# A mixture-of-experts trunk: row gathers issued two double blocks ahead, light experts begun at the sixth double block, ranking split over three steps

## The reference, cut to what matters

```python
def swiglu(h, wg, wu, wd):
    return (jax.nn.silu(h @ wg) * (h @ wu)) @ wd

def moe_swiglu(h, router, eg, eu, ed):
    t = h.reshape(b * s, d)                       # 256 x 1024
    logits = (t @ router).astype(jnp.float32)
    top_v, top_i = lax.top_k(logits, TOP_K)       # 2 of 8
    top_w = jax.nn.softmax(top_v, axis=-1)
    combine = jnp.sum(jax.nn.one_hot(top_i, N_EXPERTS) * top_w[..., None], axis=1)
    for e in range(N_EXPERTS):
        out = out + combine[:, e:e + 1] * swiglu(t, eg[e], eu[e], ed[e])
    return out
```

## Time and profile before

| | |
|---|---|
| median of 3 runs | 1368.14 us (1366.64 to 1369.67) |
| the profiled execution | 1369.39 us, span of the profile 1367.6 us |
| TensorE (PE) busy | 1323.7 us, 97% (a matmul's row includes its drain) |
| VectorE (DVE) busy | 1121.4 us, 82% |
| ScalarE (ACT) busy | 942.1 us, 69% |
| mean granted TensorE clock | 0.991 |
| chain that ended last | PE 76%, DVE 14%, DMA 5%, ACT 3% |
| DMA | 438.27 MB, mean 320 GB/s over the span; 362 to 422 GB/s in the slices from 513 to 1333 us |

### The profile page before, as it was taken

The page is one execution under the profiler, slowest core; times in us unless marked ns, Lnnn a source line. Parts: engine busy times, 40 slices in busy tenths (PEclk is TensorE's granted clock), DMA queues, the critical chain, the costliest instruction groups (busy, mean ns, idle before and its releaser), DMA issues.

```text
span 1367.6 us, 17501 instructions
## 1 busy us (share of the span) xinstructions
PE 1323.7 (97%) x6684; PEld 1098.5 (80%) x6685; DVE 1121.4 (82%) x1037; ACT 942.1 (69%) x879; POOL 95.1 (7%) x67
## 2 busy tenths in 40 slices
PE   8999999999999999999999999989999999999984
PEld 6898888887898778888887888868888778888873
DVE  5766654456666998899999999979999889999986
ACT  4644444444745877778878887868888788878773
POOL 1140000000141000000000000000000010000020
PEclk9999999999999999999999999999999999999997
DMA  9434655553433899999999999999999999999991
GB/s 351 181 120 161 216 185 184 186 213 118 160 124 139 337 344 396 382 384 396 417 416 389 421 409 419 404 362 401 421 413 410 394 406 408 411 422 414 411 421 75
DMA packets 63222, 438.27 MB, mean 320 GB/s; under 512 B 7231, under 2 KB 7409, under 8 KB 11938
## 3 DMA queue, kind: packets, MB, share of 16 engines
q1 hardware_dynamic: 58896, 423.23, 78.0%
q0 software_dynamic: 4096, 13.84, 2.7%
q10 hardware_dynamic: 146, 0.07, 0.0%
HBM read 430.83 MB, written 6.29 MB: 320 GB/s over the span
## 4 chain that ended last, share of the span: by engine, by line
PE 76%; DVE 14%; DMA 5%; ACT 3%; issue 2%; SPq 0%; DVEq 0%; ACTq 0%
PE ps L2099 31%; PE ps L2123 16%; DVE w_lo L390 8%; PE ps L2219 6%; PE ps L1787 4%; PE ps L1802 4%; DMA small<-tokens,tok_i 3%; PE ps L1890 3%; DVE spare_w L390 2%; PE ps L2228 2%; PE ps L2239 2%; PE ps L1764 2%; DMA raw<-in_stream 2%; ACT w_hi L385 2%; ACT spare_w L385 1%
## 5 line engine op out<-in xcount | busy, mean ns | idle before, releaser
L390 DVE TENSOR_TENSOR w_lo<-raw,w_hi 128x2048 fp32r<-128x2048 f32 x313 | 715.4, 2302 | 131.5 <-ACT w_hi L385 130.5
L385 ACT ACTIVATE w_hi<-raw 128x2048 fp32r<-128x2048 f32 x315 | 599.8, 1916 | 171.9 <-PE ps L2099 69.9
L2099 PE MATMUL ps<-w_hi,xT_hi 128*128 128x512 f32 x564 | 224.1, 397 | 1.9 <-DVE xT_lo L1349 1.3
L2099 PE MATMUL ps<-w_lo,xT_hi 128*128 128x512 f32 x564 | 220.1, 390 | 0.0
L2099 PE MATMUL ps<-w_hi,xT_lo 128*128 128x512 f32 x564 | 219.5, 389 | 0.0
L390 DVE TENSOR_TENSOR spare_w<-raw,spare_w 128x2048 fp32r<-128x2048 f32 x85 | 194.4, 2287 | 17.3 <-ACT spare_w L385 17.2
L385 ACT ACTIVATE spare_w<-raw 128x2048 fp32r<-128x2048 f32 x85 | 162.8, 1916 | 17.3 <-PE ps L2123 13.8
L2099 PEld LDWEIGHTS ps<-w_hi,xT_hi 128*128 128x128 f32 x564 | 106.0, 188 | 23.3 <-DVE xT_lo L1349 1.5
L2099 PEld LDWEIGHTS ps<-w_lo,xT_hi 128*128 128x128 f32 x564 | 105.8, 188 | 22.9
L2099 PEld LDWEIGHTS ps<-w_hi,xT_lo 128*128 128x128 f32 x564 | 106.1, 188 | 20.9
L2123 PE MATMUL ps<-w_hi,aT_hi 128*128 128x512 f32 x284 | 113.5, 400 | 2.6 <-DVE w_lo L390 2.6
(11 more groups left out here) (352 smaller groups left out, 1956.8 us busy)
## 6 DMA issues: line engine op xcount, KB each, us to landing
raw<-in_stream SPq DMA_DIRECT2D x400, 1024.0 KB, 7.6
outs<-work POOLq DMA_DIRECT2D x5, 512.0 KB, 8.2
gain<-in_gains POOLq DMA_DIRECT2D x4, 512.0 KB, 5.4
h<-in_x SPq DMA_DIRECT2D x2, 512.0 KB, 6.7
raw<-in_stream SPq DMA_DIRECT2D x2, 512.0 KB, 6.5
tokens<-big POOLq DMA_DIRECT2D x2, 512.0 KB, 3.8
outs<-work POOLq DMA_DIRECT2D x4, 256.0 KB, 7.1
out<-work SPq DMA_DIRECT2D x4, 256.0 KB, 3.0
```

The costliest lines, as they stand in the source:

```text
L385: nc.scalar.activation(home(n, 0), raw[:, n % RAW, :], ACT.Copy).then_inc(hi_done, 1)
L390: nc.vector.tensor_tensor(home(n, 1), raw[:, n % RAW, :], home(n, 0).bitcast(F32), ALU.subtract).then_inc(lo_done, 1)
L2099: last = nc.tensor.matmul(ps[:, 4 + s, :], (xT_hi, xT_lo)[xp][:, k, x * P:(x + 1) * P], w((n + half), wp, kk * 512, (kk + 1) * 512), start ...
```

## The change

Three things change, and a few lines follow from them.

1. `TURNS`: five heavy steps instead of ten stand ahead of the first light one. After them the row is mostly "h h l". Counted: before, 8 light steps follow two heavy ones, 9 follow a single heavy one and 1 follows the ten; after, 13 follow two, 4 follow one and 1 follows the five. The last three light steps follow a light one in both.
2. The gather's places come from a new table (`PLACE`, the dispatch's step). Ids and the gather DMA stand one step after the dispatch, as before, but the transposes stand two steps after the DMA's issue (heavy: two and three), where they stood one (one and two) after it. The ids use PSUM bank 5 instead of 4, and on TensorE they stand between the two halves of down; they wait for the second block's gate and up product to be read (`gate_up_free(1, ...)`). A light gather fetches 64 rows instead of 128.
3. `ranks` moves up in step 0 (ahead of the dispatch and the low part of unit m + 5), `crowded` goes to step 3 and `rows` to step 6.

| expert p | before: dispatch, ids, transposes, begin | after |
|---|---|---|
| 5 (light) | 4, 5, 6, 9 | 0, 1, 3, 4 |
| 1 | 1, 2, 3 and 4, 6 | 3, 4, 6 and 7, 8 |
| 2 | 12, 13, 14 and 15, 17 | 14, 15, 17 and 18, 19 |
| 6 (light) | 21, 22, 23, 26 | 20, 21, 23, 24 |
| 3 | 24, 25, 26 and 27, 29 | 24, 25, 27 and 28, 29 |
| 4 | 35, 36, 37 and 38, 40 | 35, 36, 38 and 39, 40 |
| 7 (light) | 38, 39, 40, 43 | 40, 41, 43, 44 |

```diff
-TURNS = "hhhhhhhhhhlhlhhlhlhhlhlhhlhlhlhhlhlhhlhhlhlhlhhlhhlhllll"
+TURNS = "hhhhhlhhlhhlhhlhlhhlhhlhhlhhlhhlhhlhhlhhlhlhhlhlhhlhllll"
-GATHER_AT = {BEGIN[p]: p for p in range(1, N_EXP)}
+def place_steps():
+    at, later = {}, STEPS
+    for p in reversed(BY_BEGIN[1:]):
+        at[p] = later = min(BEGIN[p] - (5 if p < HEAVY else 4), later - 2)
+    return at
+PLACE = place_steps()
+PLACE_AT = {i: p for p, i in PLACE.items()}
+IDS_AT = {i + 1: p for p, i in PLACE.items()}
+TURN_AT = {i + 3: (p, 0) for p, i in PLACE.items()}
+TURN_AT.update({i + 4: (p, 1) for p, i in PLACE.items() if p < HEAVY})
+FIRST_LOAD_AT = {BEGIN[p] - 1: p for p in range(1, N_EXP)}
...
 # gpsimd
-                pool.indirect_dma_start(small[:, D:2 * D], None, tokens[:, :],
-                                        bass.IndirectOffsetOnAxis(ap=tok_i[:, p:p + 1], axis=0)).then_inc(ga_in, 16)
+                count = P if p < HEAVY else LIGHT_ROWS
+                pool.indirect_dma_start(small[0:count, D:2 * D], None, tokens[:, :],
+                                        bass.IndirectOffsetOnAxis(ap=tok_i[0:count, p:p + 1], axis=0)).then_inc(ga_in, 16)
...
 # vector, step
-                if i + 5 in GATHER_AT:
-                    dispatch(GATHER_AT[i + 5])
+                if i == 0:
+                    ranks()
+                if i in PLACE_AT:
+                    dispatch(PLACE_AT[i])
...
-                if i == 0:
-                    ranks()
+                if i == 3:
                     crowded()
-                if i == 1:
+                if i == 6:
                     rows()
...
 # tensor
+            def gate_up_free(par, p, B, i):
                 if p < HEAVY:
-                    pe.wait_ge(fm.mul, B + 1)
+                    pe.wait_ge(fm.mul, B + par + 1)
                 else:
-                    pe.wait_ge(pair_copied, FOLDED[i] + 1)
+                    pe.wait_ge(pair_copied, FOLDED[i] + par + 1)
...
+            def bank_5_read(i):
+                if i in IDS_AT:
+                    pe.wait_ge(id_cp, GATHER_NO[IDS_AT[i]])
...
                     down(fm, 1, B, 0, m + 4, 0, j == 0, False)
+                    if i in IDS_AT:
+                        gate_up_free(1, q, B + 2, i + 1)
+                        token_ids(IDS_AT[i])
                     down(fm, 1, B + 1, 1, m + 5, 0, False, final)
```

More of the change, by code:

```diff
@@ L556, in gather @@
                     pool.wait_ge(gaT_ps, 2 * r)
-                pool.indirect_dma_start(small[:, D:2 * D], None, tokens[:, :],
-                                        bass.IndirectOffsetOnAxis(ap=tok_i[:, p:p + 1], axis=0)).then_inc(ga_in, 16)
+                count = P if p < HEAVY else LIGHT_ROWS
+                pool.indirect_dma_start(small[0:count, D:2 * D], None, tokens[:, :],
+                                        bass.IndirectOffsetOnAxis(ap=tok_i[0:count, p:p + 1], axis=0)).then_inc(ga_in, 16)
             lights_out = 0
             for i in range(STEPS):
-                if i + 4 in GATHER_AT:
-                    gather(GATHER_AT[i + 4])
+                if i in IDS_AT:
+                    gather(IDS_AT[i])
                 if i in RETURN_AT:
@@ L846, in step @@
                     ffn_block(fm, 1, B + 3, 1, m + 4)
[L847 to L851, removed]
+                if i in TURN_AT:
+                    p, g = TURN_AT[i]
+                    if p < HEAVY:
+                        gather_hi_heavy(p, g)
+                    else:
+                        gather_hi_light(p)
                 hi_unit(act, m + 7)
@@ L1455, in step @@
                 lo_unit(dve, m + 7)
[L1456 to L1462, removed]
+                if i in TURN_AT:
+                    p, g = TURN_AT[i]
+                    if p < HEAVY:
+                        gather_lo_heavy(p, g)
+                    else:
+                        gather_lo_light(p)
+                if i in IDS_AT:
+                    token_ids(IDS_AT[i])
                 if i == STEPS - 4:
@@ L2259, in token_ids @@
                 for t in range(TT):
-                    last = nc.tensor.matmul(ps[:, 4, 0:1], disp[:, t, :].bitcast(F32), token[:, t:t + 1], start=(t == 0),
+                    last = nc.tensor.matmul(ps[:, 5, 0:1], disp[:, t, :].bitcast(F32), token[:, t:t + 1], start=(t == 0),
                                             stop=(t == TT - 1), skip_group_check=True)
@@ L2331, in scatter @@
                 last.then_inc(sc_ps, 1)
-            def bank_4_free(p, B, i):
+            def gate_up_free(par, p, B, i):
                 if p < HEAVY:
-                    pe.wait_ge(fm.mul, B + 1)
+                    pe.wait_ge(fm.mul, B + par + 1)
                 else:
-                    pe.wait_ge(pair_copied, FOLDED[i] + 1)
+                    pe.wait_ge(pair_copied, FOLDED[i] + par + 1)
             def bank_4_read(i):
[L2342 to L2348, removed]
+                if i in TURN_AT:
+                    p, g = TURN_AT[i]
+                    pe.wait_ge(ga_lo, GATHER_NO[p] * 2 + (g + 1 if p < HEAVY else 2))
                 if i == STEPS - 4:
                     pe.wait_ge(slot_cp, 3)
+            def bank_5_read(i):
+                if i in IDS_AT:
+                    pe.wait_ge(id_cp, GATHER_NO[IDS_AT[i]])
             def expert_step(i):
@@ L2370, in expert_step @@
                     whole(gu)
+                    bank_5_read(i - 1)
                     whole(gate_up(fm, 1, B + 3, 1, m + 2, 0, wait_mul=p < HEAVY, q=q % 2))
@@ L2373, in expert_step @@
                     light_gate_up(q, 0, m, r)
+                    bank_5_read(i - 1)
                     light_gate_up(q, 1, m + 2)
[L2375 to L2384, removed]
+                if i in TURN_AT:
+                    x, g = TURN_AT[i]
+                    gate_up_free(0, q, B + 2, i + 1)
+                    if x < HEAVY:
+                        gather_T_heavy(x, g)
+                    else:
+                        gather_T_light(x)
                 if i == STEPS - 4:
-                    bank_4_free(q, B + 2, i + 1)
+                    gate_up_free(0, q, B + 2, i + 1)
                     last_slots()
```

6 lines of the change are left out of this document (3 added, 3 removed).

## The result

The changed kernel takes 1356.84 us (median of 4 runs, 1355.3 to 1357.76), against 1368.09 us before in the same rounds (4 runs). The ratio is 0.9911, 95% interval [0.9899, 0.9923]: 11.3 us faster by the medians, 12.2 by the ratio. The profiled execution took 1355.3 us (before 1369.39), its span is 1353.5 us (before 1367.6). The forecast was 1355.0, or 1356.3 for a profiled execution.

The account below looks back on a forecast made before the run. TensorE was taken to bound the heavy steps, with stalls from gathers and step order in the mixed stage. Terms -10.1 - 4.4 - 0.4 + 0.7 + 0.2 + 0.9 = -13.1 us gave 1355.0 us, range 1351.5 to 1361.5.

Parts of the forecast that it names:

- Clean lengths of the blocks: Mixed stage: "h h l" takes 46.30 us, "h l" 30.37; five light steps moving behind two heavy ones gain 4.4 us.
- the shape is worth nothing: Rival, chance 0.12: "h h l" blocks in a row don't keep 46.30 us, the 4.4 go, 1359.4 us.
- The gathers: DMA waits and waits after transposes in light steps: 9.8 of 11.24 us of stalls go, with expert 1's 10.1.
- the gap: Wait left after expert 3's second half of transposes in light step 28, at step 29's gate and up: 1.4 us.
- Ranking: Moving `ranks`, `crowded`, `rows`: gain of 0.4 us in steps 0 and 1, loss of 0.7 in steps 3 and 6.
- Ids: Token ids between the halves of down wait for the second block's product to be read: loss of 0.2 us in all.
- Stream: Weight loads in the mixed stage fit with 2% to spare; a few short waits cost 0.9 us.
- The rival built on it: Mixed stage, chance 0.14: the stream takes over and its rate sets the time, 1361 us at 408 GB/s.
- the slower one: Rival, chance 0.03: the stream falls back to 397 GB/s with light steps in the mix, 13 us slower, 1381 us.
- The lead doesn't help: Rival, chance 0.06: another engine would have ended the gather waits just after the DMA; only shape is left, 1364 us.
- The sum: Whole kernel: gathers, shape, ranking, ids and stream add to -13.1 us; 1356.3 us profiled, 1355.0 median.

Follow-up runs that it names:

- the two controls: Changed kernel with the row of steps of before, 1359.41 us; the same with dispatch, ids, gather and transposes also in their old steps, 1369.83 us.
- The control: Changed kernel with the old row of steps and dispatch, ids, gather and transposes in their old steps; 1369.83 us, ratio 1.0002 to the kernel before.
- the thin stream: Changed kernel with half of each down unit's load left out from the second double block on; 1352.80 us, ratio 0.9874 to the kernel before.

## Why the prediction was right, point by point

**Clean lengths of the blocks.** Right. 46.30 and 46.31 us for "h h l" in blocks that follow each other, so the rival "the shape is worth nothing" fell in the trace of the change itself, and the run with the old row of steps gives it its price, 3.75 us. The term had been sized 4.4. It left out that the gathers and ids don't cost quite the same in the two rows: 0.17 us in the stretch and 0.47 ahead of it.

**The gathers.** Right in mechanism; the sum was 10.1 us, 9.8 of it in the stretch. Measured on the old row of steps are 9.0 in the stretch (18.23 to 9.23) and 0.4 at expert 1 (its first transposes stand in a step of 17.27 us instead of 17.67). That is 9.4, 0.7 less than forecast. The 10.8 (784.92 - 774.16) of the two controls is no better measure, since it holds expert 2's late landing. The gain holds three things, which the runs tell apart only in part: the DMA waits with the slow clock behind them, the transposes that moved out of light steps (its removal for expert 3 is measured, with the ids' wait, as 2.03 us), and the ids' place. By the marks from step 11 (642.12) to step 50 (1251.93), 609.81 us with eleven blocks "h h l" and three "h l", 11 x 46.30 + 3 x 30.37 = 600.41, the same five gathers that cost 18.23 us before cost 9.40 after. Forecast were 6.99 + 1.4 = 8.4. What I had put too low is mostly expert 3. Its ids stand in the light step 25, which takes 15.99 us instead of 15.05, 0.94 more where 0.49 was counted (the row below shows 0.20 of waiting, and the matmuls take 0.61 us instead of 0.50). The second half of its transposes makes steps 28 to 30 longer by 2.25 us; less 0.47 for the transposes, the gap costs 1.8 instead of 1.4.

```profile
873.53 0.61 PE L2279 MATMUL ps<-cst,disp 128*128 128x1 f32 x4 [0.20 <-DVE act_x L1312]
```

**Ranking.** The exchange was as forecast in kind: the down of step 0 is 0.77 us longer, and step 1 loses its wait of 1.4 us (18.22 us before, 16.80 in both runs with the old row and no ids in step 1). That is a gain of 0.65, where 0.4 was forecast. The term of 0.7 us for `crowded` and `rows` in steps 3 and 6 was wrong in size: it is 0.

**Ids.** Forecast a loss of 0.2. The control's 0.15 us in all between the marks doesn't measure it, since larger parts cancel there; its two light steps with ids are 0.3 us longer each than before (15.99 and 15.97 us against 15.66 and 15.65), although the cast's wait is gone there. In the changed kernel one light step (25) has it, and step 1 waits 0.2 us, so the loss is nearer to 0.5.

**Stream.** The term of 0.9 us was wrong in size: it is 0 between the marks, as the thin stream shows. The rival built on it had 0.14 and falls; so does the slower one, which needed a rate below 405 GB/s: the stream carried 411, and a stretch of 46 us 414 with TensorE never idle. One reading of the earlier trace rows was too narrow: the 5.2 us are those of the tile `w_hi` at one line. All of ScalarE's waits for the stream come to 10.5 us before and 11.0 after, which leaves the argument as it was.

**The lead doesn't help.** Out: taking it away costs 6.8 us between the marks, with some 1.5 of them in the ids.

**The sum.** From step 0's down to step 50 the change brings 14.66 - 0.77 = 13.9 us, where 13.1 were forecast. The two losses that didn't come (0.7 and 0.9) and the better exchange of the ranking (0.25) make 1.85 us more, and the gathers with their ids about 1.0 less. That they nearly cancel is luck. The profiled time of 1355.3 is 1.0 from the 1356.3 forecast; the median of the runs is 1.8 from 1355.0, so the gain in medians is 11.3 where the traces differ by 14.1. I take that for scatter of the runs, though no run shows it: the profiled execution before was above its median, and the one after is the fastest of its four.

## What to carry to other kernels

Take the length of a repeated block from the chain's own marks and multiply it out over a long stretch: the excess is the sum of all stalls, also of those that no single row names, and a change of order can be priced with the same two block lengths. A gather whose landing varies (here 8.8 to 12.8 us) is worth issuing a whole step ahead of the step that would cover it on average, since its cost was made in the few steps that were short. Transposes and ids cost least here in the heavy steps, where the chain behind them is covered. That a queue is busy all the time doesn't make it the bound: making this one a sixth lighter changed no step from 1 to 50. And a control whose sum agrees with the kernel before can hide parts that cancel, so compare it step by step.

## What the runs showed of the hardware that I had not expected

- The gathers (GpSimd, 128 or 64 rows of 4 KB) did not land sooner in the median when the weight stream was a sixth lighter: 9.7 to 13.2 us, median 12.7, in the changed kernel with the thin stream, against 9.2 to 13.1, median 11.7, with the full one.
- A wait of TensorE of 3.68 us was followed by a half clock for some 5 us (0.52 in 894 to 900), one of 2.8 us in the run with the lead of one step by a shorter one (0.66 in the 5 us from 903), one of 2.04 us in the control too (0.75 in 706 to 712, down in 7.11 us), and one of 1.78 us by none (down in 5.48 us).
- DMA engines with a share of 1.01 moved 411 GB/s in the changed kernel; with the lighter stream the share is 0.93 at 344. So a share of 1.01 did not mean that the stage was bound by the stream: no step from 1 to 50 became shorter with the lighter one.
